# A two-block transformer forward on one core: the first five weight slabs and their activation tiles are begun two ahead of the last one landed, in place of all at once

## What is computed

```python
h = rmsnorm(x, mix_norm[l])
proj = h @ w_in[l]                       # 2048 x 7184
sq, sk, sv, gq, gk, gv, gz, gb, ga = jnp.split(proj, cuts, axis=-1)
sb_out = stick_breaking_attention(...)
gdn_out = gated_deltanet(gq, gk, gv, gz, gb, ga, ...)
x = x + jnp.concatenate([sb_out, gdn_out], axis=-1) @ w_out[l]
x = x + memory_cross_attention(rmsnorm(x, xattn_norm[l]), mem_n, ...)
x = x + conv_ffn(rmsnorm(x, ffn_norm[l]), ...)
x = rmsnorm(x, final_norm)
for i in range(2):                       # second block
    p = rmsnorm_2(x, norm_g[i]) @ w_in_i
    x = x + (attention(p) * jax.nn.silu(gate)) @ w_out_i
return rmsnorm_2(x, final_g)
```

## Time and profile before

| | before |
|---|---|
| median of 3 runs | 2189.91 us |
| lowest, highest | 2189.22, 2191.97 us |
| the profiled execution: time, span | 2189.73 us, 2187.9 us |
| PE, DVE, ACT busy | 99%, 74%, 61% |
| instructions | 34438 |
| moved by DMA | 389.31 MB, mean 178 GB/s |

### The profile page before, as it was taken

The page is one execution under the profiler, slowest core; times in us unless marked ns, Lnnn a source line. Parts: engine busy times, 40 slices in busy tenths (PEclk is TensorE's granted clock), DMA queues, the critical chain, the costliest instruction groups (busy, mean ns, idle before and its releaser), DMA issues.

```text
span 2187.9 us, 34438 instructions
## 1 busy us (share of the span) xinstructions
PE 2176.4 (99%) x13414; PEld 1880.9 (86%) x13414; DVE 1609.5 (74%) x2922; ACT 1325.0 (61%) x2555; POOL 9.7 (0%) x22
## 2 busy tenths in 40 slices
PE   9999999999999999999999999999999999999998
PEld 8888888888898888888888888888888888888887
DVE  7897655687687877755777867767677777688774
ACT  7766345775576666544666655555556655567764
POOL 0000000000000000000000000000000000000000
PEclk9999999999999999999999999999999999999999
DMA  7543333565455555555555555555555455544454
GB/s 275 173 140 117 121 121 135 187 219 200 164 176 192 191 186 190 189 189 189 191 186 191 191 185 193 183 184 183 190 170 179 164 193 193 187 160 154 147 195 142
DMA packets 107619, 389.31 MB, mean 178 GB/s; under 512 B 12304, under 2 KB 12560, under 8 KB 106688
## 3 DMA queue, kind: packets, MB, share of 16 engines
q1 hardware_dynamic: 105408, 377.37, 50.2%
q0 software_dynamic: 1904, 9.47, 1.2%
q10 hardware_dynamic: 144, 0.26, 0.0%
HBM read 384.34 MB, written 2.13 MB: 177 GB/s over the span
## 4 chain that ended last, share of the span: by engine, by line
PE 95%; DVE 2%; ACT 1%; issue 0%; DMA 0%; SPq 0%; DVEq 0%; ACTq 0%
PE main L500 87%; PE two L500 7%; PE two L503 1%; DVE WL L944 1%; DVE gt L944 0%; ACT WH L1595 0%; DMA RAW<-ws 0%; DVE GQ L950 0%; ACT PPw L1595 0%; ACT PP L1595 0%; ACT AQ L1595 0%; ACT L1594 0%; PE main L546 0%; DVE PP L950 0%; DVE FQ L944 0%
## 5 line engine op out<-in xcount | busy, mean ns | idle before, releaser
L1595 ACT ACTIVATE WH<-RAW 128x512 fp32r<-128x512 f32 x1416 | 885.8, 630 | 671.8 <-PE main L500 664.8
L944 DVE TENSOR_TENSOR WL<-RAW,WH 128x512 fp32r<-128x512 f32 x1416 | 963.2, 688 | 396.9 <-ACT WH L1595 386.8
L500 PE MATMUL main<-A,WH 128*128 128x512 f32 (+1 forms) x3680 | 1145.0, 393 | 2.2 <-DVE WL L944 2.2
L500 PEld LDWEIGHTS main<-A,WL 128*128 128x128 f32 x3584 | 673.6, 188 | 154.8
L500 PE MATMUL main<-A,WL 128*128 128x256 f32 x3584 | 713.2, 278 | 0.0
L500 PEld LDWEIGHTS main<-A,WH 128*128 128x128 f32 x3680 | 562.8, 189 | 16.3 <-issue 10.9
L500 PE MATMUL main<-H,WH 128*128 128x512 f32 x704 | 221.1, 395 | 0.0
L500 PE MATMUL main<-B,WH 128*128 128x512 f32 (+1 forms) x640 | 184.3, 373 | 0.0
L500 PEld LDWEIGHTS main<-H,WL 128*128 128x128 f32 x704 | 132.2, 188 | 31.3
L500 PE MATMUL main<-H,WL 128*128 128x256 f32 x704 | 138.3, 278 | 0.0
L500 PE MATMUL main<-WH,A 128*128 128x512 f32 (+1 forms) x448 | 137.7, 382 | 0.0
(11 more groups left out here) (301 smaller groups left out, 1718.6 us busy)
## 6 DMA issues: line engine op xcount, KB each, us to landing
RAW<-ws SPq DMA_DIRECT2D x707, 512.0 KB, 3.3
CB<-cscr POOLq DMA_DIRECT2D x4, 1024.0 KB, 5.2
XT<-xT POOLq DMA_DIRECT2D x4, 512.0 KB, 7.5
MS<-memT POOLq DMA_DIRECT2D x4, 512.0 KB, 7.6
xs<-xT SPq DMA_DIRECT2D x7, 256.0 KB, 7.9
out<-YT SPq DMA_DIRECT2D x7, 256.0 KB, 2.6
CST<-cst SPq DMA_DIRECT2D x1, 1248.0 KB, 7.5
G<-g POOLq DMA_DIRECT2D x1, 1024.0 KB, 4.9
```

Source lines behind the costliest of these rows:

```text
L500: return e.matmul(o, l, r, start=start, stop=True, skip_group_check=True)
L944: return e.tensor_tensor(o, a, b, op)
L1595: return e.activation(o, i, f, bias=bias, scale=scale, accum_out=accum)
```

## The change

Of the first slabs, slab 1 with its tiles is issued at once as before. From slab 2 on, SP first waits until the slab two before has landed, then issues the tiles and the slab: slab 2 behind the landing of slab 0, slab 3 behind slab 1, slab 4 behind slab 2. The three tile loads that follow wait as well: tiles 10, 11 for slab 3, tiles 12, 13 and tiles 14, 15 for slab 4 (`s_raw[min(i, NRAW + 1) - 2]` is `s_raw[3]`, `s_raw[4]`, `s_raw[4]`). `w.wait_ge` leaves out a wait whose value it has waited for already, so the last of them adds none.

```diff
             e.dma_start(RAW[:, 0, 512:1024], ws[0][:, 512:1024]).then_inc(s_raw[0], 16)
+
             for i in range(1, NRAW):
+                if i >= 2:
+                    w.wait_ge(s_raw[i - 2], 16)
                 load_x(i)
                 load(i)
             for i in range(NRAW, 8):
+                w.wait_ge(s_raw[min(i, NRAW + 1) - 2], 16)
                 load_x(i)
```

## The result

| | before | after |
|---|---|---|
| median (14 runs each) | 2189.91 us | 2195.05 us |
| lowest, highest | 2189.22, 2191.97 us | 2193.35, 2196.80 us |
| ratio after to before | | 1.0021, 95% interval 1.0014 to 1.0029 |
| the profiled execution: time, span | 2189.73, 2187.9 us | 2194.09, 2192.3 us |

A forecast was written before the change was run, and what follows sets the result against it. PE was taken as the bound, busy 2176.4 of 2187.9 us; 1.47 us gained at half 2, added waits hidden, took 2189.7 to 2188.3, plus 0.2 for the runs' median: 2188.4 us, range 2187.5 to 2191.5.

The forecast's parts named there:

- The bound and its place: Start of the kernel: PE idles 1.74 us before half 2, waiting for slab 1; at most 1.74 us to gain.
- Slab 1 is whole at 8.4 us: Slab 1 lands at 8.4 in place of 9.87 us; half 2 begins at 9.83, not 11.30: gain 1.47 us.
- The first rival: Slab 1's load is not held up by later ones, so no gain: 2189.9 us; chance 0.15.
- A pair then takes 3.93 us, and a hop with its wait 3.98: Tiles and slab, issue to landing: 2.03 us fixed plus 1.90 us data; 0.05 us more for SP's wait.
- "Due" times: When PE needs halves 8, 9, 10: 18.47, 19.91, 21.35 us, at 1.44 us of PE a half.
- The margins: Time to spare before PE needs the data: 0.2 us for tiles 12, 13 and 0.15 us for slab 5.
- if a hop is longer by d, slab 5 is late by 3d: Two hops and slab 5's own load add up; costs begin beyond d = 0.05, whole gain gone at d = 0.54 us.
- the slower rival: Pairs arrive too late, at half 10 behind slab 5: 2.6 us lost, 2192.5 us; slower by 0.1 to 4.4: chance 0.2.
- The gain reaches the end: The 1.47 us won at half 2 lasts: PE nearly always full, loads, ACT and DVE paced by PE from slab 6.

The follow-up runs named there:

- the first wait: Changed kernel with only the wait of slab 2 and its tiles for slab 0 kept, other four removed: 2190.34 us against 2189.87 for before.
- the run with one pair at a time: Changed kernel, but slabs 2, 3, 4 each wait for the slab directly before; tiles 10 to 15 don't wait: 2197.97 us against 2190.15 for before.
- Three ahead: Changed kernel, but each wait is for the slab three ahead in place of two: 2190.44 us against 2189.87 for before.
- a warm start: Changed kernel, but SP first loads the constants and other parameters (1.5 MB) and waits for them: 2201.24 us.
- the tiles' waits alone: Changed kernel without the waits of slabs 2 to 4; only tiles 10 to 15 wait for slabs 3 and 4: 2192.55 us against 2189.87 for before.
- the kernels with a shorter gap: Four kernels: PE kept busy in the gap 2189.99 us, slab 1 in halves 2189.50, halves with tiles 2, 3 apart 2189.41, slab 2's wait alone 2190.34.
- the run with the slabs alone: Against before: tiles 2 to 15 issued ahead of slab 1; slabs 2, 3, 4 each wait for the one two before: 2195.64 us against 2190.24.

## Why the prediction was wrong

- **The bound and its place** (half 2 waits for slab 1): right for the profile of before, and where slab 1 landed sooner, half 2 began sooner. But slab 0 landed at 7.2 to 8.4 us in five of the other profiles (6.43 before), and half 1 waited as well, for 0.3 to 1.7 us: the start varies from one execution to the next, which one profile doesn't show.
- **"Slab 1 is whole at 8.4 us"**: wrong in size. It landed at 9.43, and PE's wait fell from 1.7 to 1.2 us, not to 0.3; half 2 gained 0.44 us and not 1.47. In four kernels with the first wait or a stricter one slab 1 landed at 8.8 to 9.9, in four with its neighbours issued at once at 9.6 to 10.6. So part of it is chance. The premise fails too, that slab 1 is whole when 1.63 MB have moved at the old rate. The stretches up to the landing of slab 1, in the changed kernel and in the run with one pair at a time:

```profile
0.00:9.43 9.43, 8.24 (x36) 7.11 (x36) 3.14 (x9) 4.07 (x6) 0.20 (x4) 1.00 0.67 217
```

```profile
0.00:9.93 9.93, 6.65 (x28) 5.35 (x29) 2.96 (x9) 3.96 (x6) 0.20 (x4) 1.00 0.53 164
```

In the changed kernel 9.43 us x 217 GB/s = 2.05 MB had moved, against 2.10 before: the wait ended at 6.21, and slab 2's pair ran beside slab 1 all the same. With one pair at a time it was 9.93 x 164 = 1.63 MB, with nothing of slab 2, and slab 1 landed no sooner: fewer bytes had moved, in no less time (slab 0 also landed late there, at 8.01, and it is one execution). By the Trainium skill ("DMA: Bandwidth & Descriptors", Queues, rings and completion order) each DMA engine takes its descriptors in ring order; alone that would give 9.87 again. The first rival is nearer than my forecast, and the spread doesn't settle whether the gain is 0.4 us or nothing.
- **"A pair then takes 3.93 us, and a hop with its wait 3.98": the step that failed.** Measured: 6.2, 5.7, 6.0 us, and 5.7 from slab 4 to slab 5 where 4.6 were counted. I took the 3.3 us of a lone slab apart into 2.03 us fixed and data at 414 GB/s. But 414 GB/s is the rate of a deep queue, in which, as I read it, an engine that has not yet begun the newest transfer still has older ones to work on. With two pairs under way the DMA ran at 261 and 276 GB/s and 0.78 to 0.82 busy, with one pair and two tiles at 199 and 0.58. Three ahead landed a pair every 1.95 us again, one alone gave hops of 4.4 to 4.6 us, a warm start changed nothing. The run with one pair shows which half of the sum was off: 47 GB/s in the first 1.5 us (9.93 to 11.40), as a fixed part would have it, and then 308 GB/s (11.40 to 13.50) where 414 were counted.
- **"Due" times, 2.6 and 2.2 us from landing to PE**: right, to 0.02 us, in the changed kernel and with the tiles' waits alone.
- **The margins** of 0.15 and 0.2 us, and "if a hop is longer by d, slab 5 is late by 3d": right in kind, and decisive. The hops were longer by 2.2 and 2.0 us, the last load by 1.1, slab 0 landed 0.2 us sooner; 19.0 + 5.1 + 2.2 = 26.3 us for half 10. I had set the worst d at 1.4, from a lone slab's worst load, so the slower rival was the right mechanism with its price too low: 2.6 us, measured 3.5 at half 10.
- **"The gain reaches the end"**, and with it the loss: the loss grew. 0.9 us came behind half 10, where DVE had no stock (3.54 us late there, 4.4 from 37 us on). The profiled executions stop at 4.4 us; the medians are 5.1 us apart. The spread of the changed kernel (3.5 us) is wider, and clock falls behind a chance gap, as seen in two experiments, may be a part; the profile of the changed kernel shows none, and 2 of its 14 executions have a mean granted clock of 0.998.
- **What stays open**: why an engine starts a transfer 2.9 us after its issue when the queue is short, and takes its first packets slowly. The bytes ahead are not enough: slab 4 had at most one slab more ahead of it than slab 3, 1.27 us at 414 GB/s, and took 2.3 us longer (5.7 against 3.4). It is not the cold start. What is issued behind a load may matter and was not tested by itself.

## What to carry to other kernels

A latency measured with one transfer under way and a rate measured with many can't be joined into a price for two: count landings per microsecond at the depth that the change will leave. Before a wait is put into a queue, work out the time to spare of everything behind it; here it was 0.15 us, so the sum rested on a number known to 1 us. To bring one transfer forward, make that transfer smaller, and leave the others queued: slab 1 in two halves took 0.65 us off the median without a new wait (a difference that the interval does not separate from nothing).

## What the runs showed that I had not expected

- A gap of PE of 2.12 us at full granted clock was followed in two profiles by a stretch at 0.50 (16 matmuls in 3.00 us, 18 in 3.40). One of 1.74 us in the profile of before was not, nor those of 1.68, 1.97 and 1.59 us in the run with one pair at a time; there the clock was at 0.50 only from 24.96 us on, late in the fourth, of 2.79 us. In the run with three ahead the stretch cost 1.6 us (5.9 in place of 4.32 us for three halves), nearly as much as the gap itself.
- There are two groups of executions of the kernel before: 82 of 99 below 2191.1 us, 17 from there to 2191.97. Their distance, their clocks and the kernels with a shorter gap fit such a fall of the clock; no profile of before from the upper group shows it.
- A landing is the slowest engine's. In the run with the slabs alone fifteen engines were done with slab 4 by 19.26 us and one at 20.89, and slab 5 also waited for one, at 22.13 against 20.67.
